# First group of every stage in two passes per tile, and the forget chain spread over four steps of a decoder kernel

## The reference

```
h = x + 0.5 * rms_norm(swiglu(rms_norm(x)))            # feed-forward 1: 1024 -> 2816 -> 1024
p = rms_norm(h) @ w_in                                 # input projection
y = concat(conv A, gated linear attention B, short conv C, forgetting attention D)
h = h + rms_norm(y @ w_out)                            # output projection
h = h + 0.5 * rms_norm(swiglu(rms_norm(h)))            # feed-forward 2
```

## Time and profile before

| | |
|---|---|
| runs, median (3 runs) | 1069.25 us (1068.82 to 1069.58) |
| the profiled execution | 1069.6 us, of which the span of the trace is 1067.8 |
| TensorE busy | 1048.1 us, 98% |
| VectorE busy | 689.8 us, 65% |
| ScalarE busy | 571.1 us, 53% |
| GpSimd busy | 270.8 us, 25% |
| transfers | 187.42 MB at 176 GB/s |

### The profile page before, as it was taken

The page is one execution under the profiler, slowest core; times in us unless marked ns, Lnnn a source line. Parts: engine busy times, 40 slices in busy tenths (PEclk is TensorE's granted clock), DMA queues, the critical chain, the costliest instruction groups (busy, mean ns, idle before and its releaser), DMA issues. The chain is left out here.

```text
span 1067.8 us, 24171 instructions
## 1 busy us (share of the span) xinstructions
PE 1048.1 (98%) x8956; PEld 1019.6 (95%) x8956; DVE 689.8 (65%) x1029; ACT 571.1 (53%) x969; POOL 270.8 (25%) x338
## 2 busy tenths in 40 slices
PE   6999999999999999999999999999999999999997
PEld 5999999998989999999999999999989999999997
DVE  5666644499986666654476666446999776666443
ACT  5544454477467544454475444546665765444542
POOL 3222220113505222220142222103054232222200
PEclk9999999999999999999999999999999999999999
DMA  7665667443735665656636565764536356565561
GB/s 260 210 182 179 186 207 241 150 142 98 234 92 193 196 180 177 188 169 184 189 122 201 176 192 179 234 198 121 177 103 213 109 175 221 177 189 173 172 188 45
DMA packets 63746, 187.42 MB, mean 176 GB/s; under 512 B 9258, under 2 KB 19506, under 8 KB 63538
## 3 DMA queue, kind: packets, MB, share of 16 engines
q1 hardware_dynamic: 63666, 186.31, 56.3%
HBM read 182.90 MB, written 3.38 MB: 174 GB/s over the span
## 5 line engine op out<-in xcount | busy, mean ns | idle before, releaser
L313 DVE TENSOR_TENSOR w_lo<-raw,w_hi 128x1024 fp32r<-128x1024 f32 (+1 forms) x316 | 411.7, 1308 | 326.8 <-ACT w_hi L303 326.7
L303 ACT ACTIVATE w_hi<-raw 128x1024 fp32r<-128x1024 f32 x336 | 344.4, 1030 | 244.7 <-PE ub L347 170.9
L345 PE MATMUL ub<-hg_hi,w_hi 128*128 128x264 f32 x960 | 276.6, 288 | 0.0
L346 PE MATMUL ub<-hg_lo,w_hi 128*128 128x264 f32 x960 | 272.1, 283 | 0.0
L347 PE MATMUL ub<-hg_hi,w_lo 128*128 128x264 f32 x960 | 271.8, 283 | 0.0
L345 PE MATMUL ub<-act_hi,w_hi 128*128 128x264 f32 x704 | 200.5, 285 | 0.0
L347 PE MATMUL ub<-act_hi,w_lo 128*128 128x264 f32 x704 | 200.0, 284 | 0.0
L346 PE MATMUL ub<-act_lo,w_hi 128*128 128x264 f32 x704 | 199.1, 283 | 0.0
L345 PE MATMUL quad<-hg_hi,w_hi 128*128 128x264 f32 x688 | 196.4, 285 | 0.0
L346 PE MATMUL quad<-hg_lo,w_hi 128*128 128x264 f32 x688 | 194.9, 283 | 0.0
L347 PE MATMUL quad<-hg_hi,w_lo 128*128 128x264 f32 x688 | 194.8, 283 | 0.0
(11 more groups left out here) (250 smaller groups left out, 1308.4 us busy)
## 6 DMA issues: line engine op xcount, KB each, us to landing
raw<-in_w_gu SPq DMA_DIRECT2D x176, 512.0 KB, 4.0
raw<-in_w_dn SPq DMA_DIRECT2D x64, 512.0 KB, 4.0
raw<-in_w_in SPq DMA_DIRECT2D x44, 512.0 KB, 3.7
raw<-in_w_dn SPq DMA_DIRECT2D x32, 384.0 KB, 3.6
raw<-in_w_out SPq DMA_DIRECT2D x16, 512.0 KB, 3.7
pages<-in_cache_k SPq DMA_DIRECT2D x32, 128.0 KB, 3.2
pages<-in_cache_v SPq DMA_DIRECT2D x32, 128.0 KB, 3.1
con<-in_con SPq DMA_DIRECT2D x1, 1192.0 KB
```

Of the source, the lines that this page charges most:

```text
L303: eng.activation(w_hi[:, slot, 0:w], raw[:, slot, 0:w], ACT.Copy).then_inc(*sig("hi_ready", reps))
L313: eng.tensor_tensor(w_lo[:, slot, 0:w], raw[:, slot, 0:w], w_hi[:, slot, 0:w].bitcast(F32), ALU.subtract)\
L345: eng.matmul(out, a_hi, x_hi[:, k0 + k, :], start=(first and k == 0), stop=False)
L346: eng.matmul(out, a_hi, x_lo[:, k0 + k, :], start=False, stop=False)
```

## The change

The diff has four parts.

1. `multiply_first` waits for the rounded tile (`hg_hi` or `ym_hi`) and multiplies it with both weight parts of the three units, six matmuls; then it waits for the tile's rest (`hg_ready` or `ym_ready`) and issues the three matmuls with it.
2. The transposes of heads 2 and 3 go to the banks `ub[3]` and `mb[0]` instead of `ub[2]` and `mb[0]`, by a list of their own (`turned_bank`). The wait for the centring (`a_cen`) moves from the third head's transposes to the start of the output projection, and `conv_var` waits for the third copy of probabilities.
3. ScalarE's softplus of the forget gate moves from step 7 to step 6.
4. VectorE's four operations of the forget chain move from the head of step 9 to the ends of steps 7, 8, 9 and 10, one each, behind the level work of the step.

```
@@ -197,6 +197,7 @@
         NORM = mb[3][:, 0:NT]
         ROOT, SCALED = mb[1][:, 0:NT], (mb[2][:, 0:NT], ub[3][:, 0:NT])
         fox_bank = (mb[0], mb[1], ub[2], mb[2])
+        turned_bank = (mb[0], mb[1], ub[3], mb[0])
         taps_sum = ub[3]
 
         S = {n: ctx.enter_context(nc.semaphore(n)) for n in per}
@@ -351,20 +352,22 @@
 
             return ub[n if n < 4 else n % 2]
 
-        def multiply_first(eng, l, phase, x_hi, x_lo, banks, widths, ready, count):
+        def multiply_first(eng, l, phase, x_hi, x_lo, banks, widths, high, ready, count):
+
+            def part(w, s, k):
+                return w[:, s, k * widths[s]:(k + 1) * widths[s]]
 
             for k in range(KD):
+                eng.wait_ge(*at(l, high, count + k + 1))
                 for s in range(GROUP):
-                    m = widths[s]
                     if k == 0:
                         eng.wait_ge(S["split_done"], l * UNITS + PHASES[phase][0] + s + 1 + RING)
-                    if s == 0:
-                        eng.wait_ge(*at(l, ready, count + k + 1))
-                    a_hi, a_lo = (w[:, s, k * m:(k + 1) * m] for w in (w_hi, w_lo))
-                    out = banks[s][0:m, 0:NT]
-                    eng.matmul(out, a_hi, x_hi[:, k, :], start=k == 0, stop=False)
-                    eng.matmul(out, a_hi, x_lo[:, k, :], start=False, stop=False)
-                    mm = eng.matmul(out, a_lo, x_hi[:, k, :], start=False, stop=k == KD - 1)
+                    out = banks[s][0:widths[s], 0:NT]
+                    eng.matmul(out, part(w_hi, s, k), x_hi[:, k, :], start=k == 0, stop=False)
+                    eng.matmul(out, part(w_lo, s, k), x_hi[:, k, :], start=False, stop=False)
+                eng.wait_ge(*at(l, ready, count + k + 1))
+                for s in range(GROUP):
+                    mm = eng.matmul(banks[s][0:widths[s], 0:NT], part(w_hi, s, k), x_lo[:, k, :], start=False, stop=k == KD - 1)
                     if k == KD - 1:
                         mm.then_inc(*sig("unit_done"))
 
@@ -492,7 +495,7 @@
                     multiply_unit(pe, ub[s][:, 0:NT], s, hg_hi, hg_lo, KD, 0, True, True, reps)
 
                 pe.wait_ge(*at(l, "gu_read", f * 44))
-                multiply_first(pe, l, gu, hg_hi, hg_lo, ub, [P] * GROUP, "hg_ready", 8 * (q - 1))
+                multiply_first(pe, l, gu, hg_hi, hg_lo, ub, [P] * GROUP, "hg_hi", "hg_ready", 8 * (q - 1))
 
                 pe.wait_ge(setup, 16 * 3)
                 pe.wait_ge(*at(l, "h_acc", 9 * q))
@@ -621,7 +624,7 @@
                 mm.then_inc(*sig("a_sum"))
 
             def conv_var(l):
-                after(l, a_sq=1)
+                after(l, a_sq=1, d_pt=3)
                 for c in range(2):
                     mm = pe.matmul(ub[3][:, 0:NT], ones, a_sqr[:, c, :], start=c == 0, stop=c == 1)
                 mm.then_inc(*sig("a_var"))
@@ -642,12 +645,10 @@
 
             def fox_transposes(l, h):
                 after(l, d_pn=2 * h + 2)
-                if h == 2:
-                    after(l, a_cen=2)
                 if h == 3:
                     after(l, d_pt=1)
                 for i in range(3):
-                    mm = pe.transpose(fox_bank[h % 3][:, i * P:(i + 1) * P], sm[:, h, i * P:(i + 1) * P], ident)
+                    mm = pe.transpose(turned_bank[h][:, i * P:(i + 1) * P], sm[:, h, i * P:(i + 1) * P], ident)
                 mm.then_inc(*sig("d_pT"))
 
             def fox_outputs(l):
@@ -753,7 +754,7 @@
                     fox_scores(l, 0)
 
             def mixer(l):
-                multiply_first(pe, l, "in", hg_hi, hg_lo, ub, IN_WIDTH, "hg_ready", 0)
+                multiply_first(pe, l, "in", hg_hi, hg_lo, ub, IN_WIDTH, "hg_hi", "hg_ready", 0)
                 pe.wait_ge(*at(l, "h_acc", 9))
                 pe.matmul(NORM, ones, h_acc[:, :], start=True, stop=True).then_inc(*sig("h_sum"))
                 for n in range(GROUP, 24):
@@ -767,7 +768,8 @@
                     mix(l, n)
                 pe.wait_ge(*at(l, "proj", 24))
                 pe.wait_ge(*at(l, "d_pt", 4))
-                multiply_first(pe, l, "out", ym_hi, ym_lo, ub, [P] * GROUP, "ym_ready", 0)
+                pe.wait_ge(*at(l, "a_cen", 2))
+                multiply_first(pe, l, "out", ym_hi, ym_lo, ub, [P] * GROUP, "ym_hi", "ym_ready", 0)
                 for n in range(GROUP, KD):
                     pe.wait_ge(S["split_done"], l * UNITS + PHASES["out"][0] + n + 1 + RING)
                     if n >= 4:
@@ -883,7 +885,7 @@
 
                     after(l, b_z=1)
                     softplus(l, soft[:, :], mb[2][:, 0:NT], par[:, PAR["ba"]:PAR["ba"] + 1], "b_sp")
-                if n == 7:
+                if n == 6:
 
                     after(l, proj=2)
                     softplus(l, lft[:, :], proj[0:FGW, FG, :], par[0:FGW, PAR["bf"]:PAR["bf"] + 1], "d_sp")
@@ -1005,7 +1007,7 @@
 
             def probabilities(l, h):
                 after(l, d_pT=h + 1)
-                act.activation(smT[:, h, :], fox_bank[h % 3][:, 0:3 * P], ACT.Copy).then_inc(*sig("d_pt"))
+                act.activation(smT[:, h, :], turned_bank[h][:, 0:3 * P], ACT.Copy).then_inc(*sig("d_pt"))
 
             def mixer(l):
                 def inp(i, s, reps, lead):
@@ -1155,14 +1157,6 @@
                             dve.scalar_tensor_tensor(out, x, w, y, ALU.mult, ALU.add).then_inc(*sig("a_tap"))
 
             def mix(l, n):
-                if n == 9:
-
-                    after(l, d_sp=3, proj=2)
-                    log_sigmoid(l, lf[:, :], proj[0:FGW, FG, :], par[0:FGW, PAR["bf"]:PAR["bf"] + 1], lft[:, :], "d_lf")
-                    after(l, d_lf=2)
-                    dve.tensor_tensor_scan(cf[:, 0:TP], const("ones", TP, FGW), lf[:, 0:TP], 0.0, ALU.mult, ALU.add).then_inc(*sig("d_cf"))
-                    after(l, d_cf=1)
-                    dve.tensor_scalar(cf[:, 0:TP], cf[:, 0:TP], -8.0, None, ALU.mult).then_inc(*sig("d_cf"))
                 if n == 4:
 
                     after(l, b_z=1, b_sp=3)
@@ -1178,6 +1172,19 @@
                     level_keys(l, n - 4)
                 if 5 <= n <= 10:
                     level_exponents(l, n - 3)
+                if n == 7:
+
+                    after(l, d_sp=3, proj=2)
+                    dve.tensor_scalar(lf[:, :], proj[0:FGW, FG, :], par[0:FGW, PAR["bf"]:PAR["bf"] + 1], 0.0, ALU.add, ALU.min).then_inc(*sig("d_lf"))
+                if n == 8:
+                    after(l, d_lf=1)
+                    dve.tensor_tensor(lf[:, :], lf[:, :], lft[:, :], ALU.subtract).then_inc(*sig("d_lf"))
+                if n == 9:
+                    after(l, d_lf=2)
+                    dve.tensor_tensor_scan(cf[:, 0:TP], const("ones", TP, FGW), lf[:, 0:TP], 0.0, ALU.mult, ALU.add).then_inc(*sig("d_cf"))
+                if n == 10:
+                    after(l, d_cf=1)
+                    dve.tensor_scalar(cf[:, 0:TP], cf[:, 0:TP], -8.0, None, ALU.mult).then_inc(*sig("d_cf"))
                 if n == 11:
 
                     after(l, a_sg=1, a_z=1, proj=10)
```

32 lines of the change are left out of this document (19 added, 13 removed).

## The result

The changed kernel takes 1072.89 us (median of 8 runs, 1071.38 to 1074.08) against 1069.67 us for the kernel before on the same chip (1068.31 to 1070.21): a ratio of 1.0032, 95% interval 1.0023 to 1.0041. It is slower by 0.3%, where 1067.7 was predicted. The profiled span is 1071.7 us, 3.9 more than before.

What follows compares the result with a forecast made beforehand. TensorE, busy 98% of the span, was taken as the bound. Boundaries -1.6, mixers -0.54, output projections +0.4 and start +0.24 gave -1.5 us: 1067.7 us against a median of 1069.25, range 1066.5 to 1069.0.

Steps and rivals of the forecast that it cites:

- Downstream that much survives: Mixer after the decode queries: the 0.27 us per layer is kept, as VectorE and its two late waits move along.
- What is late next?: Mixer levels after step 9's mask: keys wait for ScalarE's decay, so 0.13 us comes back at the next mask.
- the mixer's term: Spread forget chain in the mixer's levels: 0.71 us wait goes, 0.27 remains per layer, -0.54 us in all.
- The slower rival: Mixer levels, steps 7 to 10: VectorE falls behind, TensorE waits some 0.5 us at each; 1072.3 us, chance 0.04.
- Levels: Mixer levels: step 9's mask wait of 0.71 us per layer goes, 0.13 comes back at the next mask.
- a dependent operation costs its full time wherever it stands: Rival on the mixer's forget chain: spreading saves nothing, 0.2 us more per layer, 1068.1 us; chance 0.1.
- Boundaries: Five inner stage boundaries: the gap after TensorE's filler goes, 0.325 us each, -1.6 us (bounds 1.3 to 1.9).
- a pace of 0.12 at once: Sign at the boundaries: first product starts 3.46 us after the filler's start, the next ones 0.12 us apart immediately.
- Start: Kernel start: two more products fall after the third weight's arrival, two move to the high clock side, +0.24 us.
- Output projection: Output projections: unit 0 finishes later, so a new wait before unit 4; +0.4 us for two (bounds 0 to 0.6).
- Banks: Mixer's probability transposes: the fourth set still waits for ScalarE's first copy, so TensorE leaves the step unchanged; no gain.

Runs made afterwards that it cites:

- the chain's run: Kernel before with only the forget chain spread over steps 7 to 10 and its softplus at step 6; ratio 1.0026 (1.0016 to 1.0035).

## Why the prediction was wrong

**The step that failed** is the sentence "Downstream that much survives", and the question ahead of it, "What is late next?". I followed VectorE, ScalarE and TensorE to the next thing that is late, and GpSimd stands nowhere in that working. The change makes TensorE reach the later units 0.75 to 0.92 us earlier (in the table's count), ScalarE rounds their weights earlier, and GpSimd starts its halves of unit 14 earlier by 0.94 (249.35 against 249.63, with the mark at 207.62 against 206.96), while VectorE's rest of that time moves up by only 0.13 (249.10 against 248.57). The distance of 0.12 us between a_dec and GpSimd's unit 15 was in the trace of before and was no term of the sum. Its price, with what followed, was 2.6 us per layer: the mixer's term of -0.27 a layer measured +2.04 (the 1.84 of the table and the boundary's 0.20).

The sign of it was there as well: a_pad's 128x512 took 1.77 us at 251.14, where the same shape with two inputs takes 0.68 elsewhere (L1131 in the earlier trace rows). I took 1.77 as its cost and did not ask what it stood behind. So two questions were skipped, one of the trace and one of the rule cited above.

**The slower rival** gave 1072.3, near the measured time, but by another way: it asked for some 0.5 us at each of four levels, and only the one at step 10 waits in the changed kernel, 0.17. It was a wrong mechanism with a near number. Its chance of 0.04 stood for all slower cases, which was too little for a change that moves three engines against a fourth.

**Levels, right.** L567 comes 0.55 earlier once the boundary's 0.20 is taken off: 0.71 less the new wait at step 10 (sum: 0.13, seen: 0.17).

```profile
247.84 0.28 PE L348 MATMUL ub<-hg_hi,w_lo 128*128 128x264 f32 x1
...
248.22 0.49 PE L559 MATMUL quad<-qk 32*64 32x64 f32 x32
```

0.38 from start to start, where 0.21 is normal. That only 0.27 per layer would be left at the decode queries was right with a_pad slow (0.31 left), and no law: with a_pad freed as well, the whole 0.55 arrives at the output projection (0.75 less the boundary's 0.20). The rule that a dependent operation costs its full time wherever it stands, one of my rivals, would have left 0.07; it falls. The section that the prediction cites for it (the Trainium skill, page "VectorE: DVE Perf Modes", section "The DRAIN you can't avoid") itself adds that a next operation that is not held starts earlier, and the rows agree, with 0.09 us.

**Boundaries, right in kind, a third too large** (predicted -1.6; the five stages keep -0.20, -0.30, -0.16, -0.20 and -0.32, in all -1.2). The row that answers to the earlier trace rows:

```profile
865.51 3.62 PE L535 MATMUL quad<-con 128*128 128x256 f32 x16
...
868.78 0.47 PE L366 MATMUL ub<-hg_hi,w_hi 128*128 128x264 f32 x1
869.08 0.28 PE L367 MATMUL ub<-hg_hi,w_lo 128*128 128x264 f32 x1
```

The first product starts 3.27 after the filler, not 3.46, but the second 0.30 behind it and not 0.12. From the second on it is as forecast, 3.57 against 3.58, where the kernel before had 3.92. So "a pace of 0.12 at once" was wrong and harmless. At the second product the five boundaries win 0.31, 0.30, 0.38, 0.30 and 0.35, in the mean 0.33, the sum's 0.325. What was counted at nothing is the next unit: unit 3 is not in the group, and TensorE now comes to it before VectorE has its rest. 0.1 is lost there in both mixers and 0.2 at the middle boundary, and nothing to 0.03 at the other two. (PEld rows are TensorE's weight loads.)

```profile
218.94 1.77 DVE L314 TENSOR_TENSOR w_lo<-raw,w_hi 128x1024 fp32r<-128x1024 f32 x1
...
220.77 0.19 PEld L346 LDWEIGHTS quad<-hg_hi,w_hi 128*128 128x128 f32 x1 [0.22 <-DVE w_lo L314]
...
549.54 0.19 PEld L346 LDWEIGHTS quad<-hg_hi,w_hi 128*128 128x128 f32 x1 [0.40 <-DVE w_lo L314]
```

The kernel before has no such wait of the weight load at unit 3. In the mixers this rest took 1.77, where the same shape took 1.21 at the middle boundary; it began while GpSimd was still adding squares (218.87 to 219.63). That it stood behind GpSimd is read from these rows and was not tested.

**Start, right by its mechanism, and hidden by scatter.** +0.66 in the changed kernel's profile against +0.24. From the first product with the third weight to the first boundary the new order takes 194.95 and 194.46 us where the clock rises 5.4 and 4.3 us after that product (195.03 where it rises after 5.5), the old order 194.66 to 194.72 and 194.24 at 5.4 and 4.3: 0.22 to 0.29 for the order. The rest of the 0.66 is the clock, which rose 6.1 us after it in that one run and 5.4 before, and 0.1 from the weight's arrival. Over all profiles the rise came 3.0 to 6.1 us after that product, each order on both sides of 5.

```profile
18.23 0.41 PE L367 MATMUL ub<-hg_hi,w_lo 128*128 128x264 f32 x1
18.45 0.32 PE L366 MATMUL quad<-hg_hi,w_hi 128*128 128x264 f32 x1
18.60 0.29 PE L367 MATMUL quad<-hg_hi,w_lo 128*128 128x264 f32 x1
```

This is the fall from 0.22 to 0.12 of the earlier trace rows, 0.8 later. It bears out the scatter that the prediction cited from the Trainium skill, page "TensorE: Matmul & The Clock Gate", section "What's actually happening"; the page puts it at 0.5 us to either side, and these profiles lie up to 3.1 us apart.

**Output projection, right.** 23.44 against 23.26 us, 0.18 twice (predicted 0.4 in all); unit 4 starts 0.19 after its predecessor, with 0.23 to the next product:

```profile
326.74 0.28 PE L348 MATMUL quad<-ym_hi,w_lo 128*128 128x264 f32 x1
326.93 0.39 PE L346 MATMUL ub<-ym_hi,w_hi 128*128 128x264 f32 x1
327.16 0.29 PE L347 MATMUL ub<-ym_lo,w_hi 128*128 128x264 f32 x1
```

**Banks, right.** Counted at nothing. The wait before the fourth transposes is 0.5 a layer in every run with the old banks and 0.7 in every run with the new, but with the new ones the third transposes start 0.1 earlier, and from the first head's transposes to the fourth's TensorE takes 1.86 to 1.88 us in the kernel before and in the changed one.

**Still open.** Why pm and dstat meet GpSimd in one layer of the chain's run and not in the other is only read from rows, of which dstat's lies 0.14 us from GpSimd's. Which instructions with one input can stand behind GpSimd was seen once and not followed up. How often the changed kernel takes the one or the other way over many runs was not measured.

## What to carry to other kernels

Before moving work on VectorE, or anything that sets when GpSimd starts, list the VectorE instructions near GpSimd's that have two SBUF inputs (and those with one SBUF input and many columns, since 64 columns stood once), with the distance of each to the next GpSimd instruction: distances under the size of the shift are terms of the sum, at up to one whole GpSimd instruction each, however small the VectorE instruction. One that takes much more than its shape takes elsewhere is already standing behind GpSimd. Where GpSimd has time to spare, let it wait for VectorE's short instructions that others hang on; here four such waits turned a loss of 0.3% into a gain of 0.2%.

## What the runs showed that I had not expected

- VectorE instructions of one and two columns with two SBUF inputs took 1.23 and 1.27 us beside GpSimd's halves of 1.27 each; one column with one input took 0.14. It works both ways: GpSimd's two halves took 3.54 in place of 2.54 behind VectorE's 128x1024.
- 64 columns with one SBUF input stood for 1.26 us behind a half that had begun 0.08 us earlier, and took 0.19 where they came first.
- Between two GpSimd instructions in a row VectorE gets in: in layer 0 one instruction that had stood, in layer 1 the one that had stood and the next with two inputs. Instructions with one input in PSUM were not slower there (in the kernel before the 128x264 product into proj took 0.42 at 249.71 and the mask 0.73 at 250.05, beside GpSimd's halves from 249.63).
- 0.28 us of added VectorE work per layer changed the time by nothing (0.9999), 0.56 us by 0.25%.
